# GpSimd takes the low weight parts of three stages, and the modulation sums move to other stages

## What is computed

```python
# layer 0: z slabs, then the output slabs "so"
z, xbc, dt = split(rms_norm(x) @ in_w)
y = ssd_chunked(...) + xs * d_skip
x = x + rms_norm(y * silu(z)) @ out_w
x = x + conv_ffn(x)                       # "up0", "dn0"
# layer 1: key, query and value slabs, then "ao"
x = x + diff_attention(x, k, v, ...) @ out_w
x = x + conv_ffn(x)                       # "up1", "dn1"
# second block
mod = silu(c) @ w_ada + b_ada             # 6 x 1024 sums, needed from here on
sh1, sc1, ga1, sh2, sc2, ga2 = split(mod, 6)
proj = (rms_norm(x) * (1 + sc1) + sh1) @ w_in + b_in
q, k, v, qi, ki, wi, xr, yr, gate_a, gate_b = split(proj)
merged = sigmoid(gate_a) * (attn @ w_o_attn) + sigmoid(gate_b) * (rnn @ w_o_rnn)
h = x + ga1 * (merged @ w_out)            # "woa", "wor", "wout"
xn = rms_norm(h) * (1 + sc2) + sh2        # then "up2", "dn2"
```

## Time and profile before

| | us |
|---|---|
| median of 3 runs | 1342.14 |
| lowest, highest | 1337.2, 1342.37 |
| the profiled execution, its own time | 1342.82 |
| its span in the trace | 1341.1 |
| TensorE busy | 1213.4 (90%) |
| VectorE busy | 937.3 (70%) |
| ScalarE busy | 723.8 (54%) |
| GpSimd busy | 56.5 (4%) |
| TensorE's granted clock, mean | 0.935 |

### The profile page before, as it was taken

How to read it: one execution, slowest core, us unless ns; L and a number is a source line. 1 busy time by engine, 2 the same in 40 slices (tenths; PEclk the granted TensorE clock), 3 DMA queues, 4 the chain that set the end, 5 groups by cost and what they waited for, 6 DMA issues and landing times.

```text
span 1341.1 us, 24512 instructions
## 1 busy us (share of the span) xinstructions
PE 1213.4 (90%) x9392; PEld 1177.2 (88%) x9392; DVE 937.3 (70%) x1701; ACT 723.8 (54%) x1079; POOL 56.5 (4%) x115
## 2 busy tenths in 40 slices
PE   5998888989999979987899999899769798999997
PEld 4998877989999978876899999798758698999996
DVE  4876887778787677665787876638765566877743
ACT  5665565365554355554566553447774435765631
POOL 1000000100001101100000001000000000000000
PEclk9898898999999988886899999798898898999998
DMA  6553233655556845431455557442322343555450
GB/s 247 171 181 116 99 105 110 242 188 175 174 178 228 273 158 204 144 131 38 148 208 183 176 197 271 152 170 108 128 108 95 126 158 126 189 188 178 159 196 32
DMA packets 37184, 216.49 MB, mean 161 GB/s; under 512 B 4799, under 2 KB 7280, under 8 KB 15728
## 3 DMA queue, kind: packets, MB, share of 16 engines
q1 hardware_dynamic: 26352, 185.77, 39.9%
q0 software_dynamic: 8112, 26.75, 5.8%
q10 hardware_dynamic: 2640, 2.87, 0.6%
HBM read 214.30 MB, written 1.07 MB: 161 GB/s over the span
## 4 chain that ended last, share of the span: by engine, by line
PE 69%; DVE 15%; ACT 9%; issue 3%; DMA 2%; DVEq 0%; ACTq 0%
PE ps L596 63%; DVE wl L390 3%; ACT wh L383 3%; DMA ada_w<-in_w_ada 1%; DVE work L1418 1%; DVE ada_w L1384 1%; PE ps L683 1%; PE ps L771 1%; DVE small L1764 1%; PE ps L760 1%; DVE work L1646 1%; DVE xl L1412 1%; PE ps L673 1%; PE ps L867 1%; DVE work L1758 1%
## 5 line engine op out<-in xcount | busy, mean ns | idle before, releaser
L596 PE MATMUL ps<-xh,wl 128*128 128x256 f32 x1784 | 519.9, 291 | 15.7 <-DVE xl L1412 9.2
L596 PE MATMUL ps<-xl,wh 128*128 128x256 f32 x1784 | 514.6, 288 | 0.0
L596 PE MATMUL ps<-xh,wh 128*128 128x256 f32 x1784 | 513.9, 288 | 0.0
L390 DVE TENSOR_TENSOR wl<-raw,wh 128x2048 fp32r<-128x2048 f32 (+1 forms) x178 | 400.9, 2254 | 133.9 <-ACT wh L383 133.9
L596 PEld LDWEIGHTS ps<-xh,wl 128*128 128x128 f32 x1784 | 353.4, 198 | 21.7 <-issue 16.4
L383 ACT ACTIVATE wh<-raw 128x2048 fp32r<-128x2048 f32 (+1 forms) x178 | 333.5, 1877 | 60.4 <-PE ps L596 52.1
L596 PEld LDWEIGHTS ps<-xl,wh 128*128 128x128 f32 x1784 | 353.0, 198 | 0.5 <-issue 0.2
L596 PEld LDWEIGHTS ps<-xh,wh 128*128 128x128 f32 x1784 | 352.6, 198 | 0.0
L596 PE MATMUL ps<-actr,wh 128*128 128x256 f32 x1888 | 342.6, 284 | 0.0
L596 PEld LDWEIGHTS ps<-actr,wh 128*128 128x128 f32 x1888 | 296.5, 193 | 0.1
L596 PE MATMUL ps<-actr,wl 128*128 128x256 f32 x944 | 270.1, 286 | 3.1 <-DVE wl L390 1.8
(11 more groups left out here) (242 smaller groups left out, 1057.1 us busy)
## 6 DMA issues: line engine op xcount, KB each, us to landing
raw<-in_up SPq DMA_DIRECT2D x66, 1024.0 KB, 4.9
ada_w<-in_w_ada POOLq DMA_DIRECT2D x96, 256.0 KB, 4.5
raw<-in_xbc SPq DMA_DIRECT2D x12, 1024.0 KB, 4.9
raw<-in_z SPq DMA_DIRECT2D x8, 1024.0 KB, 4.9
raw<-in_so SPq DMA_DIRECT2D x8, 1024.0 KB, 4.9
raw<-in_dn0a SPq DMA_DIRECT2D x8, 1024.0 KB, 5.7
raw<-in_dn1a SPq DMA_DIRECT2D x8, 1024.0 KB, 5.6
raw<-in_dn2a SPq DMA_DIRECT2D x8, 1024.0 KB, 4.9
```

What stands on the lines that cost most here:

```text
L390: nc.vector.tensor_tensor(wl[:, b % RING, 0:n], raw[:, b % RING, 0:n], wh[:, b % RING, 0:n].bitcast(F32), ALU.subtract).then_inc(lo_done, 1)
L596: mm = nc.tensor.matmul(o, l, r, start=start and n == 0, stop=stop and n == 2)
```

## The change

GpSimd gets a function `low_parts` that goes through lists of streams (`pool_streams`) and computes their low parts with the same subtraction, each slab in instructions of 512 columns. It waits until the low part before is counted, since `lo_done` is one counter for both engines. VectorE's `lo` leaves those streams out, and waits for `lo_done` where its own turn begins again. The table `ADA` is new: 8, 12, 4, 12, 2, 4 and 3 slots with a pair of sums, and the first three slots of dn0 with a second pair. The transfers for the sums are sent in four parts around the low parts. The modulation vector is finished in two halves, the second behind wout.

```diff
@@ -206,9 +206,9 @@
 
 
 
-ADA = {**{f"z{half}{gr}": 1 for gr in range(4) for half in "ab"}, "so": 5, "dn0": 10,
-       **{f"{w}{s}": 1 for w in "kv" for s in range(4)}, "q0": 1, "q1": 1, "q2": 1, "q3": 1, "ao": 3, "dn1": 10}
-assert sum(ADA.values()) == 48
+ADA = {"so": 8, "dn0": 12, "ao": 4, "dn1": 12, "woa": 2, "wor": 4, "wout": 3}
+ADA_MORE = {"dn0": 3}
+assert sum(ADA.values()) + sum(ADA_MORE.values()) == 48
 
 
 def repeat(eng, n, stage, lag=0, rolled=True, between=None):
@@ -229,6 +229,17 @@
     else:
         for s in range(n + lag):
             stage(s // RING, s % RING)
+
+
+def pool_streams():
+
+    return ([f"z{half}{gr}" for gr in range(4) for half in "ab"], [f"{w}{s}" for s in range(4) for w in "kqv"],
+            ["qb", "kk", "kiv", "qi"] + [f"{w}{s}" for s in range(4) for w in ("yr", "xr")]
+            + [f"g{w}{s}" for w in "ab" for s in range(4)])
+
+
+BY_POOL = [name for part in pool_streams() for name in part]
+QUARTER = SLOT // 4
 
 
 def inside(i, j, back, n):
@@ -567,22 +578,55 @@
             nc.gpsimd.memset(blk[64:128, 64:128], 1.0).then_inc(const_done, 1)
             pool.wait_ge(lo_done, 2)
             pool.dma_start(cact[:, :], io["c"].to_broadcast([P, D])).then_inc(c_in, 16)
-            for a in range(96):
-                if a >= ARING:
-                    pool.wait_ge(ada_used, a - ARING + 1)
-                pool.dma_start(ada_w[:, a % ARING, :], io["w_ada"][a // 2][:, 512 * (a % 2):512 * (a % 2) + 512])\
-                    .then_inc(ada_in[a % ARING], 16)
-
-            pool.wait_ge(acc_done, 7 * 5)
-            step.add(nc.gpsimd.memset(mneg, 0.0))
-            step.wait()
-            nc.gpsimd.affine_select(out=mneg, in_=mneg, pattern=[[-1, T]], compare_op=ALU.is_ge,
-                                    fill=NEG, base=P, channel_multiplier=1).then_inc(mask_done, 1)
-
-            pool.wait_ge(xl_done, 8 * 6)
-            wait_misc(pool, "wi")
-            pool.dma_start(wri[:, 0, :], io["w_rg"]).then_inc(wri_in, 16)
-            pool.dma_start(wri[:, 1, :], io["w_ig"]).then_inc(wri_in, 16)
+
+            def modulation_weights(first, last):
+
+                for a in range(first, last):
+                    if a >= ARING:
+                        pool.wait_ge(ada_used, a - ARING + 1)
+                    pool.dma_start(ada_w[:, a % ARING, :],
+                                   io["w_ada"][a // 2][:, 512 * (a % 2):512 * (a % 2) + 512])\
+                        .then_inc(ada_in[a % ARING], 16)
+
+            def low_parts(part, at=None, then=None):
+
+                for name in part:
+                    for s in range(PL.N[name]):
+                        b = PL.S[name] + s + LEAD
+                        pool.wait_ge(lo_done, b)
+                        pool.wait_ge(hi_done, b + 1)
+                        for q in range(PL.size[b] // QUARTER):
+                            cols = slice(QUARTER * q, QUARTER * q + QUARTER)
+                            ins = nc.gpsimd.tensor_tensor(wl[:, b % RING, cols], raw[:, b % RING, cols],
+                                                          wh[:, b % RING, cols].bitcast(F32), ALU.subtract)
+                        ins.then_inc(lo_done, 1)
+                    if name == at:
+                        then()
+
+            def mask():
+
+                pool.wait_ge(acc_done, 7 * 5)
+                step.add(nc.gpsimd.memset(mneg, 0.0))
+                step.wait()
+                nc.gpsimd.affine_select(out=mneg, in_=mneg, pattern=[[-1, T]], compare_op=ALU.is_ge,
+                                        fill=NEG, base=P, channel_multiplier=1).then_inc(mask_done, 1)
+
+            def gate_weights():
+
+                pool.wait_ge(xl_done, 8 * 6)
+                wait_misc(pool, "wi")
+                pool.dma_start(wri[:, 0, :], io["w_rg"]).then_inc(wri_in, 16)
+                pool.dma_start(wri[:, 1, :], io["w_ig"]).then_inc(wri_in, 16)
+
+            in_ssm, in_attention, in_second = pool_streams()
+            modulation_weights(0, ARING)
+            low_parts(in_ssm)
+            modulation_weights(ARING, 46 + ARING)
+            low_parts(in_attention)
+            modulation_weights(46 + ARING, 78 + ARING)
+            mask()
+            low_parts(in_second, "qb", gate_weights)
+            modulation_weights(78 + ARING, 96)
 
 
 
@@ -1367,8 +1411,12 @@
 
             def lo(name, s):
                 ada(name, s)
-                split_lo(dve, PL.S[name] + s + LEAD)
+                if name not in BY_POOL:
+                    split_lo(dve, PL.S[name] + s + LEAD)
                 ada(name, s)
+                if s < ADA_MORE.get(name, 0):
+                    ada(name, s)
+                    ada(name, s)
 
             ada_n = [0]
 
@@ -1671,6 +1719,7 @@
             step.wait()
             step.add(V.tensor_scalar(negl, negl, -LAM_INIT, None, ALU.add))
             step.add(V.tensor_scalar(sgs, vec("subln"), 1.0 - LAM_INIT, None, ALU.mult))
+            dve.wait_ge(lo_done, PL.S["so"] + LEAD)
             residual("so", 1, 8, lambda s: [(s, PL.G["so"] + s, 0, 1)])
 
             def ffn(f, norm_args, r, scale=None):
@@ -1830,20 +1879,25 @@
                     inverse_rms("os", s - 2, orms, orinv_done)
             head_norm("or", 3, qf, sgs, on_done)
             output_low(3)
+            dve.wait_ge(lo_done, PL.S["ao"] + LEAD)
             residual("ao", 3, 4, tiles_two("ao"))
             ffn(1, ("n3", [(4, lambda m: vec("ffn_ln1", m), None)], 3, ("ao", 3)), 3)
 
-            dve.wait_ge(ada_used, 96)
             halves = ada_sum[:, :].rearrange("p (n two) -> p n two", two=2)
-            step.add(V.tensor_tensor(mod, halves[:, :, 0], vec("b_ada", 0, 48), ALU.add))
-            step.wait()
-            step.add(V.tensor_tensor(mod, mod, halves[:, :, 1], ALU.add))
-            step.wait()
+
+            def modulation(a, b):
+
+                dve.wait_ge(ada_used, 2 * b)
+                step.add(V.tensor_tensor(mod[:, a:b], halves[:, a:b, 0], vec("b_ada", a, b - a), ALU.add))
+                step.wait()
+                step.add(V.tensor_tensor(mod[:, a:b], mod[:, a:b], halves[:, a:b, 1], ALU.add))
+                step.wait()
+
+            modulation(0, 24)
             step.add(V.scalar_tensor_tensor(gs1, mod[:, 8:16], 1.0, vec("g_mix", 0, 8), ALU.add, ALU.mult))
 
             step.add(V.tensor_scalar(vec("b_ga", 0, 16), vec("b_ga", 0, 16), 0.5, None, ALU.mult))
             step.add(V.tensor_scalar(mod[:, 16:24], mod[:, 16:24], 0.5, None, ALU.mult))
-            step.add(V.scalar_tensor_tensor(gs2, mod[:, 32:40], 1.0, vec("g_ffn", 0, 8), ALU.add, ALU.mult))
             step.wait()
             norm("n4", [(5, lambda m: gs1[:, m:m + 1], None)], 4, ("dn1", 11))
             g = PL.G["wi"]
@@ -2004,6 +2058,7 @@
                     if it:
                         lo(f"{'ga' if it < 4 else 'gb'}{it%4}", 0)
 
+            dve.wait_ge(lo_done, PL.S["woa"] + LEAD)
             for s in range(2):
                 lo("woa", s)
                 for t in range(4):
@@ -2029,6 +2084,9 @@
                     V.tensor_tensor(ml[:, m, :], gaf[:, m, :], mh[:, m, :].bitcast(F32), ALU.subtract)\
                         .then_inc(ml_done, 1)
             residual("wout", 5, 4, tiles_two("wout"), lambda m: mod[:, 16 + m:17 + m])
+            modulation(24, 48)
+            step.add(V.scalar_tensor_tensor(gs2, mod[:, 32:40], 1.0, vec("g_ffn", 0, 8), ALU.add, ALU.mult))
+            step.wait()
             ffn(2, ("n5", [(6, lambda m: gs2[:, m:m + 1], None)], 5, ("wout", 3)), 5, lambda m: mod[:, 40 + m:41 + m])
             norm("n6", [(7, lambda m: vec("g_final", m), None)], 6)
 
```

## The result

The changed kernel takes 1357.9 us (median of 4 runs, 1355.6 to 1359.1) against 1339.7 for the kernel before: 1.0121 of its time, 95% interval 1.0101 to 1.0141. That is slower by more than the bound of 0.5%, for which the forecast gave 0.31, and 11.9 us above its likeliest time of 1346, though inside the range of 1326 to 1362. The change itself was forecast as 4 us and is 18.3 in these medians, 15.5 between the two traces (1341.1 and 1356.6 us); the kernel before has a median of 1339.7 us here and had 1342.1 in the runs that the forecast started from. All intervals leave out one execution of z1_one_piece, which took 1934.25 us at a granted clock of 0.554.

What follows compares the result with a forecast made beforehand. TensorE, busy 90% of the span, was taken as the bound; relieved stages could give only its idle time and lowered clock. 1342.8 + 20 (added sums) − 4 (z) − 8.5 (attention) − 4 (second block), less 0.7: 1346 us, range 1326 to 1362.

Steps and rivals of the forecast that it cites:

- z: Recurrence with z slabs: relieving VectorE gives at most 13 us, holds beside GpSimd's pieces leave 4 us of gain.
- Attention: Key, query and value loop: moving low parts and sums shortens TensorE's waits and restores clock, 8.5 us gain, bounds 4 and 12.
- Second block: Top-k and gate stages: fewer low parts give 8 us, held taps and products take back 4; gain 4, bounds 2 and 8.
- dn0: First three slots hold four sums, each buffer refill takes 5.1 us, TensorE waits: 13 us added, bounds 6 and 18.
- Ends and norms: Added sums cost 3 us in dn0's and dn1's last slots, 2.4 in norms, 1 in woa, wor and wout.
- long pieces: Rival: GpSimd's pieces exceed 1.44 us and can't keep up with dense slabs; at 2.0 us, 1362 us; chance 0.19.
- the refill: Rival: a sum's buffer comes back in 4.3 us, so dn0 costs 6 in place of 13; 1338 us, chance 0.15.
- VectorE was held off: Rival said GpSimd's pieces don't hold VectorE off, so the relieved stages give 30.5 us: 1332 us, chance 0.28.

Runs made afterwards that it cites:

- z1_one_piece: As e2, but GpSimd computes each low part in one subtraction of 2048 columns in place of four of 512: 1367.0 us.
- a1: The changed kernel, but VectorE computes the low parts beside z again; the table of sums stays as changed: 1346.7 us.
- e2: As e1, but GpSimd computes the eight low parts beside z: 1365.5 us.
- e1: The changed kernel with every low part on VectorE, keeping the new table of sums and the modulation vector in two halves: 1353.6 us.
- u1: The kernel before, with thirteen short stretches behind its output running VectorE instructions of one kind alone or beside GpSimd's subtractions or memsets; its time says nothing.
- f2: As f1, but GpSimd computes the low parts of the key, query and value slabs and of yr0 to gb3 (28 slabs): 1325.5 us.
- f1: The changed kernel with all low parts on VectorE and a new table without sums beside z and the attention: 1334.7 us.
- f3: As f2, but the low parts beside the first key, query and value slabs stay on VectorE: 1326.3 us.
- e4: As e1, but GpSimd computes the 22 low parts of qb to gb3: 1347.0 us.
- t1: As e1, but the second pair of sums of dn0's first three slots goes to qb and kk: 1336.5 us.
- d1: As t1, but each of the six sums in dn0's first three slots is done twice over the same buffer: 1340.5 us.

## Why the prediction was wrong, step by step

Two steps failed, each by about as much: what GpSimd's pieces hold on VectorE in z (6.7 us), and what a sum costs that stands ahead of a stage's end (6.9 us at the ends of dn0, dn1 and wout). The sum was 1342.8 + 20 − 4 − 8.5 − 4, less 0.7. Here is each term with what it measured (from the stages; differences between test kernels where one isolates it).

- **z: −4 forecast, +2.7 measured.** This is the first step that failed. The sums that left are worth 8.5 us, and for GpSimd's low parts the price is 9.7 to 11.6 (after and a1, e2 and e1). The forecast counted holds of four pieces in the first half of a group, which the trace has (4.6 us forecast, 3.3 + 1.1 measured), and put only 1.8 us for the second half, because its scalings have one SBUF input. They are held for 4.2 us a half, and u1 shows that this is a property of the scaling between SBUF operands. Counted as held, each slab costs VectorE 4.2 to 4.4 us for the 3.4 it was freed of, and z comes out above where it began, as it did. By size it is an estimate: 2.4 us more in each of four groups would be 9.6 us, and z missed by 6.7.
- **Attention: −8.5 forecast, −8.7 measured**, with the wrong reason. I had put it to ScalarE's and VectorE's order of high and low part. e1 keeps all low parts on VectorE and has 7.2 of it, e2 8.6. GpSimd seems to give some 2 net, which isn't clear of the spread; it loses 2.6 to 5.4 in the first slabs (f2 and f1, after and e1), which the forecast did not have, and gains more behind them, as f3 shows. That the number came out is luck.
- **Second block: −4 forecast, −2.1 measured** (yr, xr and g), at its lower bound, and of a size that single traces hardly tell (e4 less e1: 1.5). In one step the taps met six pieces and not one: 8.55 us for six.
- **dn0: 13 forecast; 14.3 measured** for the three slots (e1 less t1), with the sums' starts within 1 us of the forecast ones. This part was right, and t1 and d1 show the reason right.
- **Ends and norms: 3 + 2.4 + 1 forecast, more measured.** This is the second step that failed. TensorE's waits for the norms' squares grew by 10.6 us in all (4.5, 5.8 and 4.0 behind dn0, dn1 and wout, for 1.5 or 1.6 each). Sums in dn0's last two slots and the norm cost 3.1 (t1 less f1, one slot of two), wout 3 to 4, and the first slab after dn0 1.2 (9.7 us to the second in e1, 8.4 before). The forecast counted the sum's own 0.6 us ahead of the late low part, and for slot 10 a sum that starts at a fixed distance. It left out that the sum stands ahead of the additions to x and that its wait for the transfer, 3.6 us in dn1, falls on them whole. How long that wait is was chance: dn1's row is +4.3 us in the changed kernel and 0.0 in e2 and a1, with the same program there.

By stage the terms were short by 6.7 us in z, 1.9 in the second block, 1.1 in dn0 with its end and its norm (15.7 forecast, 16.8 measured), 2.8 at dn1's end, 3.0 at wout and 0.4 in the norms after so and ao (1.2 forecast, 1.6 in the rows from so to up0 and from ao to up1), and long by 0.2 in the attention: 15.7 us. The xbc stage, which nothing touches, ran 4.2 us shorter at the higher granted clock, which leaves 11.5, about the miss of 12.0 between the sum of 1346.3 and the traced execution of 1358.3. That it was no larger is luck too. Of the rivals, none had it: GpSimd's pieces took 1.32 us, near the forecast 1.2 and under the 1.44 from which long pieces were to decide, the refill was as slow as forecast, and VectorE was held off more, not less. The rival that was missing is that more instructions are held than those with two inputs.

## What to carry to other kernels

Before work goes from VectorE to GpSimd, list which VectorE instructions stand beside it: those with two SBUF inputs, and scalings from SBUF to SBUF, are held for as long as GpSimd works, and here a slab freed 2.2 us and held 3.7. Separate the parts of such a change in the forecast and on the chip: in z the whole gain, and in the attention most of it, came from the small sums that left the same queue, while GpSimd's low parts cost some 11 us in z and helped in the attention and behind it (f2 is 9 us below f1). And an instruction that waits for a transfer is as long as the transfer, so it belongs where what stands behind it in the queue isn't wanted soon, neither four to a slot nor ahead of a stage's last additions.

## What the hardware showed that was not expected

- A scaling (tensor by a scalar of each partition) of 128x128 f32 from SBUF to SBUF takes 0.206 us alone and was held for about 1 us by each of GpSimd's pieces (14.57 us for 32 in place of 6.6), and by eight memsets for 1.7 us in all. From PSUM it took 0.26 us beside pieces; no row has it alone.
- A product of two SBUF tensors is held by GpSimd's subtractions (15.13 us for 6.55), not by its memsets (6.55).
- GpSimd's subtraction of 512 columns takes 1.23 us, of 2048 columns 4.47, and is hardly slowed by VectorE's short instructions (1.27 us beside products), but takes turns with VectorE's subtractions of a slab (3.3 us each).
- One piece of 4.7 us or four of 1.35 made no difference that the times can tell (1367.0 and 1365.5 us).
- Untouched stages of kernels with the same program differ by up to 5 us in single traces (xbc 93.4 to 97.6 us; k, q and v 141.7 to 147.2), mostly in TensorE's busy time, at granted clocks of 0.91 to 0.96 and 0.82 to 0.86.
